# A two-block transformer kernel on one core: memory order, refined norms, local keys, state products and the sparse attention's reciprocals

## What is computed

```
block 1:  h    = norm(x) @ w_in, cut into the operands of three branches
          rwkv = gated linear recurrence (RWKV7) of 8 heads, states 64x64, in chunks of 64
          loc  = attention over a sliding window of 128 with a sink, 8 query heads of 64
                 on 2 key heads, queries and keys normed and rotated (rope)
          mem  = cross attention, 4 heads of 128, keys and values from the memory:
                 km = norm(memory @ Wk), vm = memory @ Wv
          x    = x + gate * (rwkv, loc, mem) @ w_out
block 2:  dsa  = attention over the 128 highest scored keys of each query (a mask),
                 softmax by exp and a reciprocal of the sum
          conv = causal depthwise convolution over time, 31 taps
          x    = x + (dsa, conv) @ w_out, cross attention, FFN with conv (2816)
out = final norm(x)
```

## Time and profile before

| | |
|---|---|
| median of 3 executions | 1643.43 us (1643.31 to 1647.04) |
| the profiled execution | 1643.51 us, its span 1641.7 us |
| PE busy | 1583.8 us, 96% of the span |
| DVE busy | 1102.5 us, 67% |
| ACT busy | 412.2 us, 25% |
| POOL busy | 135.1 us, 8% |

### The profile page before, as it was taken

The page is one execution under the profiler, slowest core; times in us unless marked ns, Lnnn a source line. Parts: engine busy times, 40 slices in busy tenths (PEclk is TensorE's granted clock), DMA queues, the critical chain, the costliest instruction groups (busy, mean ns, idle before and its releaser), DMA issues.

```text
span 1641.7 us, 23947 instructions
## 1 busy us (share of the span) xinstructions
PE 1583.8 (96%) x9234; PEld 1139.8 (69%) x9234; DVE 1102.5 (67%) x2163; ACT 412.2 (25%) x799; POOL 135.1 (8%) x125
## 2 busy tenths in 40 slices
PE   7999999999999999999999999999999999999997
PEld 7875544457776776777654566468876888888885
DVE  5986957954444454577859897366768787886453
ACT  3334274521111011320235566310301000000000
POOL 0020020030000000000019500000000000000000
PEclk9999999999999999999999999999999999999998
DMA  7212111111111101232211222122022222223231
GB/s 263 77 65 77 52 52 52 52 39 41 40 40 40 54 26 66 71 123 109 77 64 65 80 84 83 63 77 78 18 87 76 78 102 77 100 81 91 90 90 64
DMA packets 48721, 121.63 MB, mean 74 GB/s; under 512 B 5408, under 2 KB 19488, under 8 KB 48352
## 3 DMA queue, kind: packets, MB, share of 16 engines
q1 hardware_dynamic: 47520, 116.41, 20.8%
q10 hardware_dynamic: 864, 2.37, 0.4%
q0 software_dynamic: 224, 1.31, 0.2%
HBM read 117.98 MB, written 2.10 MB: 73 GB/s over the span
## 4 chain that ended last, share of the span: by engine, by line
PE 79%; DVE 17%; ACT 2%; issue 2%; DMA 0%; POOL 0%; DVEq 0%; ACTq 0%; POOLq 0%
PE bank L612 14%; PE bank L752 6%; PE opair L1321 4%; PE vpair L1321 4%; PE abank L1321 3%; PE bank L1321 3%; DVE arena L1881 3%; PE vpair L642 3%; PE opair L642 3%; PE abank L1073 2%; PE vpair L1073 2%; PE opair L1350 2%; DVE arena L1872 2%; PE vpair L1350 2%; DVE tmp L1872 2%; PE abank L642 2%
## 5 line engine op out<-in xcount | busy, mean ns | idle before, releaser
L612 PE MATMUL bank<-h,ring 128*128 128x512 f32 x560 | 255.5, 598 | 0.2 <-ACTq L1464 0.2
L612 PEld LDWEIGHTS bank<-h,ring 128*128 128x128 f32 x560 | 103.2, 191 | 115.3 <-issue 111.7
L1872 DVE TENSOR_TENSOR arena<-ring 128x512 f32<-128x512 f32 (+2 forms) x148 | 88.8, 600 | 71.1 <-DMA ring<-weights 44.3
L1872 DVE TENSOR_TENSOR arena<-arena,vpair 128x256 f32<-128x256 f32 x87 | 36.6, 421 | 137.9 <-PE vpair L1073 81.9
L612 PE MATMUL bank<-arena,ring 128*128 128x512 f32 (+1 forms) x320 | 122.1, 523 | 1.4 <-ACT arena L1468 1.4
L1881 DVE SCALAR_TENSOR_TENSOR arena<-arena,cols 128x512 f32<-128x512 f32 (+1 forms) x129 | 94.8, 735 | 4.6
L612 PEld LDWEIGHTS bank<-arena,ring 128*128 128x128 f32 x320 | 58.6, 193 | 42.8 <-issue 36.6
L2828 POOL TENSOR_TENSOR arena<-arena 128x512 f32<-128x512 f32 x47 | 61.7, 1312 | 10.5 <-ACT arena L1742 6.9
L1872 DVE TENSOR_TENSOR arena<-arena 128x256 f32<-128x256 f32 (+1 forms) x114 | 57.6, 505 | 6.0 <-PE bank L971 2.2
L1675 ACT ACTIVATE arena<-abank 128x256 f32<-128x256 f32 x40 | 15.4, 384 | 152.0 <-PE abank L1073 152.0
L2807 POOL TENSOR_TENSOR arena<-arena,cst 128x256 f32<-128x256 f32 x40 | 31.4, 785 | 250.8 <-DVE arena L1872 124.5
(11 more groups left out here) (374 smaller groups left out, 3195.4 us busy)
## 6 DMA issues: line engine op xcount, KB each, us to landing
ring<-weights SPq DMA_DIRECT2D x169, 512.0 KB, 3.7
ring<-weights SPq DMA_DIRECT2D x36, 256.0 KB, 3.3
ring<-weights SPq DMA_DIRECT2D x68, 128.0 KB, 2.3
x<-xt SPq DMA_DIRECT2D x8, 512.0 KB, 7.4
ring<-weights SPq DMA_DIRECT2D x40, 64.0 KB, 2.0
out<-h SPq DMA_DIRECT2D x8, 256.0 KB, 2.0
cst<-cst_in ACTq DMA_DIRECT2D x1, 1056.0 KB, 8.0
arena<-mem2t POOLq DMA_DIRECT2D x1, 1024.0 KB, 5.1
```

What stands on the lines that cost most here:

```text
L612: last = mm(o[:, 0:n], weight(), src, start=c == 0, stop=c == len(srcs) - 1)
L1872: do(V.tensor_tensor(out, a, b, op), sig)
```

## The change

Five edits, none of which changes the result but for rounding.

A. The order in which the memory's tiles are taken becomes 4, 5, 6, 7, 0, 1, 2, 3 on ACT, DVE and PE alike (`MEM_ORDER`), in the squares, the gain, the sum of squares, the memory's keys and values and the rescaling. The transfers stay as they are.

B. `rinv_refined` takes two operations in place of four; ACT squares y0 (`rinv_square(i)`, into buffers `SP` and `PT`) behind each refined exp, and signals DVE only after it.

C. The rope queries go to i = 0, 1, 2, 5; both keys are made at i = 3 from one product over all 128 partitions and four partial products, then two sums of 64 partitions and four copies of 64 partitions: eleven operations in one place instead of fourteen in two.

D. In the recurrence the o bank's chunk products stand before the v bank's; for t = 1 and 2 and the second half, one of the two pieces of dense work before the state products goes between the products of chunk 0 and those of chunk 1 (`fill(work)` at c == 0; for t = 0 that iteration is skipped, so nothing moves there).

E. In the sparse attention the reciprocal of job i stands in iteration i, behind two taps, and two more taps follow it (one from i = 14). The tap total is unchanged, 75.

```diff
-            for i in range(KD):
-                act.wait_ge((mem_in if i < 4 else mem_late_in).sem, 16)
+            for i in MEM_ORDER:
+                act.wait_ge((mem_in if i < 4 else mem_early_in).sem, 16)
                 do(fn(mem_squares[:, i, :], mem[:, i, :], ACT.Square), square_ready)
...
-                tt(t, y, y, MUL)
-                tt(t, t, mean_square(i)[:, 0:n], MUL)
-                ts(t, t, -0.5, 1.5, MUL, ADD)
-                tt(t, t, y, MUL)
+                stt(t, rinv_square(i)[:, 0:n], -0.5, mean_square(i)[:, 0:n], MUL, MUL)
+                stt(t, t, 1.5, y, ADD, MUL)
...
-                    do(fn(slot(i)[:, 0:n], slot(i)[:, 0:n], ACT.Exp, bias=col(out_bias), scale=-0.5), rinv_ready)
+                    do(fn(slot(i)[:, 0:n], slot(i)[:, 0:n], ACT.Exp, bias=col(out_bias), scale=-0.5), act_chain if refined else rinv_ready)
+                    if refined:
+                        do(fn(rinv_square(i)[:, 0:n], slot(i)[:, 0:n], ACT.Square), rinv_ready)
...
-            def rope_key(s):
-
-                own = slice(HD * s, HD * s + HD)
-                for u_ in range(2):
-                    rotated_sine(tmp[:, 1], skn, HD * u_, HD * s)
-                    tt(tmp[HD * u_:HD * u_ + HD, 0], skn[own, :], trig[own, 1], MUL)
-                tt(skd[:, s, :], tmp[:, 0], tmp[:, 1], ADD, rope_done)
+            def rope_key_products():
+
+                for s in range(2):
+                    rotated_sine(tmp[:, 1], skn, HD * s, HD * s)
+                tt(tmp[:, 0], skn, trig[:, 1], MUL)
+
+            def rope_key_sums():
+
+                halves_ = slice(0, HD), slice(HD, P)
+                for s in (1, 0):
+                    own, other = halves_[s], halves_[1 - s]
+                    tt(tmp[own, 0], tmp[own, 0], tmp[own, 1], ADD)
+                    copy(skd[own, s, :], tmp[own, 0])
+                    copy(skd[other, s, :], tmp[own, 0], rope_done)
...
-                after[1 + i] = lambda i=i: rope_query(i)
+                after[(0, 1, 2, 5)[i]] = lambda i=i: rope_query(i)
...
+            after[3] = lambda: (rope_key_products(), rope_key_sums())
...
+                    o = take_pair("o")
+                    chunk_gram(o, 0, k, kk)
+                    for last in gram(o, 1, bb, r):
+                        o_done.inc(last)
                     o = take_pair("v")
                     chunk_gram(o, 0, bb, kk)
                     for last in chunk_gram(o, 1, kk, bb):
                         v_done.inc(last)
-                    o = take_pair("o")
-                    chunk_gram(o, 0, k, kk)
-                    for last in gram(o, 1, bb, r):
-                        o_done.inc(last)
...
-                    fill(work, 2)
+                    fill(work, 1 if hb and 0 < t < NT - 1 else 2)
...
+                    if c == 0 and t < NT - 1:
+                        fill(work)
...
-            after.update({i: (lambda i=i: conv_taps(4 if i < 16 else 3)) for i in range(SEL, 25)})
-            attention(sparse_jobs(), CROSSKV, [None] * 12, sparse_fills, after, first=0, outputs=False)
+            after.update({i: (lambda: conv_taps(2)) for i in range(SEL, 25)})
+            later = {i: (lambda i=i: conv_taps(2 if i < 14 else 1)) for i in range(SEL, 25)}
+            attention(sparse_jobs(), CROSSKV, [None] * 12, sparse_fills, after, first=0, outputs=False, later=later)
```

More of the change, by code:

```diff
@@ L818, in next_h, with dense_tokens_pairs @@
                 pe.wait_ge(h_ready.sem, state["h"])
-            def dense_tokens_pairs(src, tiles, n=P, normed=False):
+            def dense_tokens_pairs(src, tiles, n=P, normed=False, order=range(KD)):
                 o = dense_bank()
@@ L824, in dense_tokens_pairs @@
                 for t in range(tiles):
-                    for c in range(KD):
+                    for i, c in enumerate(order):
                         if normed and t == 0:
                             next_h()
-                        last = mm(o[:, t * n:(t + 1) * n], src[:, c, tok(t)], w[c][:, 0:n], start=c == 0, stop=c == KD - 1)
-                        if t == tiles - 1 and c == KD - 1:
+                        last = mm(o[:, t * n:(t + 1) * n], src[:, c, tok(t)], w[c][:, 0:n], start=i == 0, stop=i == KD - 1)
+                        if t == tiles - 1 and i == KD - 1:
                             end_group(last)
-                        if c % 4 == 3:
+                        if i % 4 == 3:
                             yield
@@ L967, in memory_keys @@
                 for n in range(2):
-                    for c in range(KD):
+                    w = [weight() for _ in range(KD)]
+                    for i, c in enumerate(MEM_ORDER):
                         if g == 0 and n == 0:
                             next_h()
-                        last = mm(o[:, n * M:(n + 1) * M], weight(), memg[:, c, :], start=c == 0, stop=c == KD - 1)
-                        if g == 1 and n == 1 and c < KD - 1:
+                        last = mm(o[:, n * M:(n + 1) * M], w[c], memg[:, c, :], start=i == 0, stop=i == KD - 1)
+                        if g == 1 and n == 1 and i < KD - 1:
                             h_used.inc(last)
@@ L979, in _ @@
             pe.wait_ge(total_ready.sem, state["total"])
-            single("a", con("ones"), mem_squares[:, 0, :], M)
+            single("a", con("ones"), mem_squares[:, MEM_ORDER[0], :], M)
             memory_keys(1)
             for n in range(4):
-                for _ in dense_tokens_pairs(memg, 2, normed=n == 0):
+                for _ in dense_tokens_pairs(memg, 2, normed=n == 0, order=MEM_ORDER):
                     pass
@@ L1911, in add_square, with add_squares_of @@
                     tt(to, to, part, ADD, total_ready if i == last else dve_chain)
+            def add_squares_of(of, order):
+                st["square"] += 1
+                for i in order[1:]:
+                    st["square"] += 1
+                    dve.wait_ge(square_ready.sem, st["square"])
+                    to = of[:, order[0], :]
+                    tt(to, to, of[:, i, :], ADD, total_ready if i == order[-1] else dve_chain)
             def rinv_in(i, n=T):
@@ L2004, in rope_keys, with attention @@
                         tt(dst[64 * u_:64 * u_ + 64, :], tmp[rows, 0], tmp[rows, 1], ADD, rope_done if u_ else dve_chain)
-            def attention(jobs, stage_=(), todo=(), fills=even_fills, after={}, first=99, outputs=True):
+            def attention(jobs, stage_=(), todo=(), fills=even_fills, after={}, first=99, outputs=True, later={}):
                 n = len(jobs)
@@ L2042, in attention @@
                         signal_now(v_read)
-                    if 1 <= i <= n and not outputs:
-                        U = len(jobs[i - 1][2])
-                        s = st["exp"] % 4
-                        st["exp"] += 1
-                        dve.wait_ge(exp_done.sem, st["exp"])
-                        do(V.reciprocal(small[:, s, 8:8 + U], small[:, s, 4:4 + U]), den_ready)
-                        counted_by_act(p_ready)
                     for j in scored_in(i, n, first):
@@ L2081, in attention @@
                         after[i]()
+                    if i < n and not outputs:
+                        U = len(jobs[i][2])
+                        s = st["exp"] % 4
+                        st["exp"] += 1
+                        dve.wait_ge(exp_done.sem, st["exp"])
+                        do(V.reciprocal(small[:, s, 8:8 + U], small[:, s, 4:4 + U]), den_ready)
+                        counted_by_act(p_ready)
+                    if i in later:
+                        later[i]()
                 read_through(reading, stage_, 4 * len(stage_))
@@ L2103, in _ @@
             scaled_keys(0)
-            for i in range(KD - 1):
+            for i in MEM_ORDER[:-1]:
                 st["used"] += 1
```

23 lines of the change are left out of this document (14 added, 9 removed).

## The result

The changed kernel takes 1627.95 us in the median of four executions (1627.53 to 1628.56), the kernel before 1643.39 (1643.31 to 1647.04): a ratio of 0.9905, 95% interval 0.9892 to 0.9917. The prediction was 1626.8, range 1620 to 1634. Run again later beside others, the unaltered changed kernel took 1629.75 (1629.53 to 1630.24), so that a microsecond of the agreement is not worth much, and single terms have to be read from the traces.

A forecast was written before the change was run, and what follows sets the result against it. PE was taken as the bound, executing matmuls in 96% of the span, all but 57.9 us. The terms -1.0 - 4.4 - 5.1 - 3.9 - 2.35 = -16.75 us took 1643.51 to 1626.8 us, range 1620 to 1634.

The forecast's parts named there:

- A, -1.0: Start: PE begins about 1.0 us earlier, at 8.5 us, waiting for the first weight panel instead of the memory's tiles.
- the bound's: Start: gain 0 if the second weight panel becomes the wait, -2.3 us if the first lands after 5.3 us.
- B, -4.4: Refined norms: the 3.15 us wait and its 1.8 us slow stretch go, a new 0.55 to 0.65 us wait comes.
- C, -5.1: Local attention: the 3.85 us wait and its 1.8 us slow stretch go, some 0.55 us more waiting after the first query.
- D, -3.9: Recurrence: three waits of 0.60 us and two of 1.05 us go, 3.9 us in all; bounds +3.9 and -3.9.
- The split: Recurrence: dense work of 1.8 us ahead of chunk 1's state products removes two waits of 1.05 us, -2.1 us.
- The swap: Recurrence, end of a tile: o products ahead of the v products fill three waits of 0.60 us, -1.8 us.
- the cover: Recurrence: v products come 0.98 us later in eight sets, priced at nothing because dense work follows; 7.8 us if all exposed.
- E, -2.35: Sparse attention: gates come 1.55 us earlier once and 0.8 more from i = 14 on; DVE is full there.
- its lower bound: Sparse attention: at most -7.9 us, from 8.1 us of waits less 1.9 without DVE work ahead, plus a 1.7 slow stretch.

The follow-up runs named there:

- the kernel with the split undone: The changed kernel with the recurrence's dense work all ahead of the state products again, the order of o and v products kept as changed: median 1631.28 us.
- the nine taps behind: The changed kernel with three taps for each i throughout and the last nine behind the sparse attention: median 1627.30 us, against 1629.75 for the unaltered one beside it.

## Why the prediction was right

The total was off by 1.15 us, and that is better than its terms: two of them missed by 3.6 us together, and a stretch that nobody forecast gave 1.7 back by luck. Against the table of stretches:

- **A, -1.0: right at the start, lost again by 45 us in the first profile.** The start moved by 1.12 us, by the step as stated (PE waits for the first weight panel at 8.4), but by 45 us the kernel was 0.18 us late. The step that failed is the bound's: it looked at the second panel, which was in time, and not at the third, which lands at 18.39 us in place of 16.55 because ACT, done earlier, issues earlier. It also took 0.27 us for each matmul of the first pass, the mean of 0.43 and 0.22, and the share of the slow ones varies by up to 1.5 us in all.
- **B, -4.4: right, with a path that differs in part.** -4.26: the wait of 3.15 became 0.20, its slow stretch went, the new wait at the sums of squares is 0.51 (0.55 to 0.65 forecast). Undoing B brings wait and stretch back. The four norms of xq became 6.5 us shorter on DVE (16.41 to 9.91, from start to start), not 4.7, because the second no longer meets POOL and the third has one slow operation, of 1.64 us, in place of two. Against it DVE begins 0.84 us later, behind ACT's first square, and loses 2.6 us between the second and the third norm, 1.53 of them to a wait for weights; so its chain ends 3.06 us earlier, just enough for PE.
- **C, -5.1: right.** -4.92, with the new wait at 0.79, 0.62 more than before (0.55 forecast), and none at i = 4 or 5; undoing C brings back the wait of 3.9. Two copies of 64x512 take 0.88 us (0.43 each was taken) and the bundle 6.8, as forecast. The trace of before did have copies within SBUF, of 128x256 in 0.29 us against 0.42 for two sources, which could have told the cheaper price from the dearer.
- **D, -3.9: half wrong.** The split was taken at -2.1 and gives -1.85. The swap was taken at -1.8 "since the o products need nothing of that", and costs 0.3. What failed is the cover: I looked at what the moved products wait for, not at what the dense work behind them waits for (DVE's next operation, with some 0.2 us to spare), and I priced the v products' delay of 0.98 us at nothing, where it costs 0.15 per set of products.
- **E, -2.35: right in size and in mechanism.** -2.36: the gates came 1.3 us earlier once (1.55 forecast) and 1.1 more at the end (0.8 forecast), with DVE's load as the bound. The waits' sum fell only from 8.1 to 7.5 because in the kernel before a slow stretch had filled 1.7 us of it; without one it is 9.8 with E undone.
- **Not forecast: -1.7** from a slow stretch near 355 us of the kernel before (granted clock 0.71 from 355 to 360) that the changed kernel lacks. It is not explained by any of the edits: the kernel with the split undone has the same code up to there as the changed one, and has it.

So A and D together gave 3.6 us less than their 4.9, the lucky stretch 1.7 more, and the rest came out; that is 14.7 us up to the last wait, and the medians differ by 15.4. The forecast's statement that E's gain is small because DVE is full was the useful one: it names what more would help, fewer taps ahead of the last gate, and the nine taps behind show it. One term of it fell: a slow stretch was counted into its lower bound, and in this stage such a stretch was absorbed by later waits in both profiles that had one (before, and C undone).

## What to carry to other kernels

A removed wait was worth here about the slack of the next thing that waits for the same engine's chain (0.60 us removed, some 0.2 of slack, 0.26 won): before moving work in front of it, read how far ahead of its need that engine's next result was. In a stage where one engine is full, moving its work about inside the stage moves the other's waits about; only taking work out from ahead of the last gate shortens it. And a change of a microsecond should be read from marks in the traces of several kernels, and beside an unaltered kernel measured together with it, since here even the unaltered kernel's median moved by 1.8 us.

## What the runs showed of the hardware

The same wait does not leave the same slow stretch. Behind a wait of 3.14 or 3.15 us the two next groups of eight lost 1.8 us in one kernel and 3.0 in another; the windows of 5 us that hold them in the kernel before:

```profile
115.00:120.00 5.00, 2.67 (x8) 2.23 (x9) 3.67 (x8) 1.26 (x2) 0.00 (x0) 0.82 0.00 0
120.00:125.00 5.00, 5.00 (x19) 4.00 (x18) 1.96 (x4) 0.00 (x0) 0.00 (x0) 0.84 0.00 0
```

and with B undone the clock there is 0.68 and 0.63. Waits of 1.94 us, the last of the sparse attention, left full clock in six profiles, among them both of the changed kernel, and a stretch that cost 1.7 us in six others with the same code behind it; with E undone:

```profile
1010.00:1015.00 5.00, 3.07 (x27) 2.60 (x27) 0.00 (x0) 2.12 (x5) 0.00 (x0) 1.00 0.44 149
1015.00:1020.00 5.00, 5.00 (x14) 2.20 (x11) 0.00 (x0) 0.54 (x2) 0.00 (x0) 0.66 0.01 3
```

The wait of 2.19 us, behind which twelve matmuls took 4.44 us in the kernel before, left none with E undone. In the stage where DVE is the bound the two stretches of this kind cost nothing, since they only filled later waits. What decides between them I could not find; no experiment varied it alone. A single stretch of 1.6 to 3 us is as large as the effect of most edits here.

The start varies too. Here are the same 2.5 us in the kernel before and with A undone, about 3 to 5.5 us after PE's first matmul:

```profile
12.50:15.00 2.50, 2.50 (x13) 2.19 (x13) 2.29 (x7) 0.13 (x1) 0.00 (x0) 1.00 1.03 411
```

```profile
12.50:15.00 2.50, 2.50 (x7) 1.99 (x6) 2.32 (x6) 0.00 (x0) 0.00 (x0) 1.00 1.04 415
```

PE gets through 13 matmuls in one and 7 in the other. The pace differs by a factor of two, as between the two levels of the clock, but the clock column reads 1.00 in both, so that the column does not show what happens at the start; the starts of the matmuls do. The first 32 take 8.6 to 10.1 us by this alone.
